# Mixer and gate weights split once beside the feed-forward quads and kept in DRAM; ten instead of twelve buffers for weight tiles; another order of stores and loads

## What is computed

```python
x = x + 0.5 * swiglu(rms_norm(x, ffn1_norm), ffn1_w_gu, ffn1_w_down)      # D_FF = 2816
h = rms_norm(x, mix_norm)
q, k, v, u = split(h @ w_in)                       # 8 query heads, 2 kv heads of 64, pool width 512
a = sliding_window_attention(norm(q), norm(k), v, rel_bias, sinks)        # window 128
m = multiscale_pool(u, pool_w, pool_scale)
x = x + concatenate([a, m]) @ w_out
x = x + 0.5 * swiglu(rms_norm(x, ffn2_norm), ffn2_w_gu, ffn2_w_down)
gate = sigmoid(rms_norm(x, ple_norm) @ ple_w_gate + ple_b_gate)
e = rms_norm(p @ ple_w_proj, ple_post_norm)
return x + gate * e
```

## Time and profile before

| | us |
|---|---|
| median of 3 runs | 1740.52 (1740.1 to 1742.68) |
| the profiled execution, its time | 1737.11 |
| the profiled execution, its span | 1735.3 |
| PE busy | 1684.5 (97% of the span) |
| DVE busy | 1255.8 (72%) |
| ACT busy | 698.6 (40%) |
| POOL busy | 233.7 (13%) |

### The profile page before, as it was taken

One profiled execution on the slowest core, in us unless ns is written; L12 is line 12 of the kernel. 1 busy time (PEld: TensorE's weight loads), 2 busy tenths in 40 slices (PEclk: granted clock), 3 DMA queues, 4 the chain that ended last, 5 costly groups with the idle time before them and its releaser, 6 DMA issues.

```text
span 1735.3 us, 20459 instructions
## 1 busy us (share of the span) xinstructions
PE 1684.5 (97%) x7348; PEld 1371.6 (79%) x7348; DVE 1255.8 (72%) x1794; ACT 698.6 (40%) x1121; POOL 233.7 (13%) x245
## 2 busy tenths in 40 slices
PE   6999999999899999999999999999999999999998
PEld 4878877888788888776677788888888888888877
DVE  6888686767756768687877788777667755676785
ACT  5533232322345444356655443232223234534442
POOL 0012222222100000044140001221212300000000
PEclk9999999999999999999999999999999999999999
DMA  8135554554579765121123213454445439876533
GB/s 292 55 140 188 176 194 174 214 176 176 176 239 317 218 193 161 61 63 58 42 66 121 87 64 128 176 189 169 169 159 188 164 128 302 273 243 190 167 105 121
DMA packets 127784, 282.95 MB, mean 163 GB/s; under 512 B 10523, under 2 KB 52164, under 8 KB 119364
## 3 DMA queue, kind: packets, MB, share of 16 engines
q1 hardware_dynamic: 124376, 275.57, 47.4%
q10 hardware_dynamic: 3308, 6.08, 0.9%
HBM read 204.52 MB, written 78.66 MB: 163 GB/s over the span
## 4 chain that ended last, share of the span: by engine, by line
PE 61%; DMA 15%; DVE 13%; POOL 5%; ACT 4%; issue 3%; SPq 0%; ACTq 0%; DVEq 0%; POOLq 0%
PE bank L861 20%; PE bank L862 19%; PE bank L863 19%; DMA wdr<-in_wd 9%; POOL wdr L843 5%; DMA wdc<-wdr 3%; DVE qb L1902 1%; DVE hn L1521 1%; PE bank L1107 1%; ACT probs L1445 1%; DVE w_lo L1736 1%; DVE probs L1914 1%; DVE dn_lo L1728 1%; DMA e_dram<-et 1%; DMA e_dram<-e_acc 1%
## 5 line engine op out<-in xcount | busy, mean ns | idle before, releaser
L861 PE MATMUL bank<-h_hi,t_hi 128*128 128x512 f32 x704 | 274.9, 390 | 0.5 <-ACT p L1239 0.5
L862 PE MATMUL bank<-h_lo,t_hi 128*128 128x512 f32 x704 | 273.9, 389 | 0.0
L863 PE MATMUL bank<-h_hi,t_lo 128*128 128x512 f32 x704 | 273.9, 389 | 0.0
L843 POOL TENSOR_TENSOR wdr<-wdr 128x256 f32<-128x256 f32 x176 | 168.7, 959 | 748.0 <-DMA wdr<-in_wd 737.6
L1728 DVE TENSOR_TENSOR dn_lo<-d_f,dn_hi 128x1024 fp32r<-128x1024 f32 x154 | 185.1, 1221 | 116.0 <-ACT dn_hi L1256 115.7
L861 PE MATMUL bank<-dn_hi 128*128 128x512 f32 x616 | 241.1, 391 | 0.6 <-DVE dn_lo L1728 0.6
L862 PE MATMUL bank<-dn_lo,dn_hi 128*128 128x512 f32 x616 | 239.7, 389 | 0.0
L863 PE MATMUL bank<-dn_hi,dn_lo 128*128 128x512 f32 x616 | 239.7, 389 | 0.0
L861 PE MATMUL bank<-c_hi,t_hi 128*128 128x512 f32 x544 | 213.0, 392 | 10.4 <-DVE c L1600 9.0
L1256 ACT ACTIVATE dn_hi<-d_f 128x1024 fp32r<-128x1024 f32 x154 | 159.9, 1056 | 151.7 <-DMA d_f<-in_wd 78.2
L862 PE MATMUL bank<-c_lo,t_hi 128*128 128x512 f32 x544 | 212.2, 390 | 0.0
(11 more groups left out here) (163 smaller groups left out, 2491.2 us busy)
## 6 DMA issues: line engine op xcount, KB each, us to landing
raw<-in_gu SPq DMA_DIRECT2D x44, 1024.0 KB, 6.0
d_f<-actc SPq DMA_DIRECT2D x154, 256.0 KB, 3.2
actc<-acts SPq DMA_DIRECT2D x20, 1792.0 KB, 7.8
raw_m<-in_units SPq DMA_DIRECT2D x52, 512.0 KB, 4.1
wdr<-in_wd SPq DMA_DIRECT2D x44, 512.0 KB, 5.4
wdc<-wdr SPq DMA_DIRECT2D x44, 512.0 KB, 3.4
d_f<-wdc SPq DMA_DIRECT2D x88, 256.0 KB, 3.2
d_f<-in_wd SPq DMA_DIRECT2D x66, 256.0 KB, 4.4
```

What stands on the lines that cost most here:

```text
L843: pool.tensor_tensor(blocks[to], blocks[one], blocks[two], ALU.add).then_inc(wd_made, 1)
L861: pe.matmul(ps, whi, vhi, start=first, stop=False, skip_group_check=onto)
L862: pe.matmul(ps, whi, vlo, start=False, stop=False, skip_group_check=onto)
L863: return pe.matmul(ps, wlo, vhi, start=False, stop=last, skip_group_check=onto)
```

## The change

Four things:

1. The 26 distinct `units` tiles of mixer and gate are split once. SP loads one per turn in turns 2 to 19 of feed-forward 1 and 2 to 9 of feed-forward 2 (`split_load`), ACT rounds it at the end of its quad and DVE subtracts it in the next quad, and SP stores both halves (2 x 512 KB) into a DRAM tensor `hl` in the next turn (`split_store`). Mixer and gate then load hi and lo ready made (2 x 512 KB for each of the 52 uses), straight into the four slots; ACT and DVE have no weight work there.
2. `TR` goes from 12 to 10; the freed 8 KB hold `unit_f`/`unit_low` (one place) and `unit_rounded`.
3. In a turn, `act_store` comes first, then `split_store`, then the piece of e; the turns with two chunks become 6, 8, 12, 14.
4. At the start, the small constants are loaded ahead of x, the second projection tile is split later, the projection's result has 8 instead of 4 buffers (`NET`), and the first norm sum comes after the fifth tile. In the quads, DVE adds the e tile later in its order.

```diff
-TR = 12
+TR = 10
-WD_TWO = (6, 10, 14, 17)
+WD_TWO = (6, 8, 12, 14)
+NET = 8
+N_SPLIT = N_IN + 2 * KT
+SPLITS = [list(range(N_IN + KT)), list(range(N_IN + KT, N_SPLIT))]
...
             def unit_load(n):
-                if n >= NRAW:
-                    sp.wait_ge(unit_split, n - NRAW + 1)
-                sp.dma_start(raw_m[n % NRAW][:, 0:size], src).then_inc(raw_in[n % NRAW], 16)
+                if slot_free(n):
+                    sp.wait_ge(main_made, slot_free(n))
+                else:
+                    sp.wait_ge(gu_made, NGU if n < U_GATE else 2 * NGU)
+                    sp.wait_ge(unit_out, 32 * (len(SPLITS[0]) if n < U_GATE else N_SPLIT))
+                s = (n - U_MIX) % SLOTS
+                sp.dma_start(plain(w_hi[s][:, :]), hl[mix_unit(n) - W_IN][:, 0:UNIT]).then_inc(w_in[s], 16)
+                sp.dma_start(plain(w_lo[s][:, :]), hl[mix_unit(n) - W_IN][:, UNIT:2 * UNIT]).then_inc(w_in[s], 16)
+
+            def split_load(u):
+                if u:
+                    sp.wait_ge(unit_out, 32 * u)
+                sp.dma_start(unit_f[:, :], units[W_IN + u]).then_inc(unit_in, 16)
+
+            def split_store(u):
+                sp.wait_ge(unit_lo, u + 1)
+                sp.dma_start(hl[u][:, 0:UNIT], plain(unit_rounded[:, :])).then_inc(unit_out, 16)
+                sp.dma_start(hl[u][:, UNIT:2 * UNIT], plain(unit_low[:, :])).then_inc(unit_out, 16)
...
+                    if q % 2 == 0:
+                        act_store(ph, q // 2 - 1)
+                    if 0 < q - U_QUAD <= len(SPLITS[ph]):
+                        split_store(SPLITS[ph][q - U_QUAD - 1])
                     if ph == 0 and 0 <= q - E_QUAD <= 2 * KT:
                         n = q - E_QUAD
...
-                    if q % 2 == 0:
-                        act_store(ph, q // 2 - 1)
...
-                    for c in WD_TURN.get(q, ()):
-                        wd_chunk(ph, c)
+                    for j, c in enumerate(WD_TURN.get(q, ())):
+                        wd_load(ph, c)
+                        if j == 0 and 0 <= q - U_QUAD < len(SPLITS[ph]):
+                            split_load(SPLITS[ph][q - U_QUAD])
+                        wd_store(ph, c)
...
+            def round_unit(u):
+                act.wait_ge(unit_in, 16 * (u + 1))
+                act.activation(unit_rounded[:, :], unit_f[:, :], ACT.Copy).then_inc(unit_hi, 1)
...
                     gate1(ph, q)
                     if ph == 0 and 0 <= q - E_QUAD < 2 * KT:
                         e_squares(q - E_QUAD)
+                    if 0 <= q - U_QUAD < len(SPLITS[ph]):
+                        round_unit(SPLITS[ph][q - U_QUAD])
...
+                if 0 <= q - U_QUAD - 1 < len(SPLITS[ph]):
+                    split_unit(SPLITS[ph][q - U_QUAD - 1])
...
-                if kind in ("win", "wout") and SLOTS <= MIXU_AT[step] + LATE:
-                    m = MIXU_AT[step] + LATE
-                    if m < N_MIXU:
-                        round_unit(U_MIX + m)
```

More of the change, by code:

```diff
@@ L58 @@
 W_GATE = W_OUT + KT
-NRAW = 2
 N_MIXU = 2 * N_IN + 2 * KT
@@ L65 @@
 LAG = 5
-LATE = SLOTS - 1
 P1, P2, Q6, Q7, Q5, Q4, Q3 = range(7)
@@ L259, with program @@
 H_AT = {2: 0, 3: 1, 6: 2, 7: 3}
-def program(nc, xT, pT, units, gu, wd, poolw, small, const, onehot, rel, band_row, band, e_dram, actc, wdc, x1, out):
+def program(nc, xT, pT, units, gu, wd, poolw, small, const, onehot, rel, band_row, band, hl, e_dram, actc, wdc, x1, out):
     with ExitStack() as ctx:
@@ L1198, in round_s @@
                     act.wait_ge(gu_made, ph * NGU + FIRST)
-                elif what == ("s", Q5, 0) and ph == 0:
-                    for i in range(4):
-                        act.wait_ge(e_out[i], 16 * (2 * KT // 4))
+                elif what == ("h", 1, 0) and ph == 0:
+                    for i in range(NET):
+                        act.wait_ge(e_out[i], 16 * (2 * KT // NET))
                 act.activation(operand("hi", what), source(what), ACT.Copy).then_inc(s_rounded, 1)
@@ L1366, in _ @@
             round_pj(0)
[L1367 removed]
             act.wait_ge(small_in, 16)
[L1369 to L1370 removed]
             for n in range(2 * KT):
                 e_tile(n)
[L1373 to L1383 removed]
+                if n == 0:
+                    x_square(0, 0)
+                    x_square(0, 1)
+                    round_pj(1)
+                elif n < 4:
+                    x_square(0, 2 * n)
+                    x_square(0, 2 * n + 1)
+                elif n == 4:
+                    std(0)
+                elif n in (5, 6):
+                    round_first(0, n - 5)
+                    if n == 6:
+                        round_first(0, 2)
+                elif n - 7 < KT:
+                    round_s(0, "h", 0, n - 7)
+                else:
+                    round_first(0, 3)
             act.wait_ge(band_made, 1)
@@ L1693, in quad @@
                 todo = [(q + 1, s) for s in LOS1] if more else []
-                if ph == 0 and 0 <= q - E_QUAD - 1 < 2 * KT:
-                    e_accumulate(q - E_QUAD - 1)
                 if q == 2:
                     split_t(ph, *todo[0])
-                if more:
+                elif more:
                     add_t(ph, q + 1, 0)
@@ L1708, in quad @@
                 make_w3(ph, q)
-                for x in todo[1:3]:
+                for x in todo[1 + (q == 2):3]:
                     split_t(ph, *x)
@@ L1991, in build @@
     x1 = nc.dram_tensor("x1", (D_MODEL, SEQ), F32, kind="Internal").ap()
-    program(nc, xT, pT, units, gu, wd, poolw, small, const, onehot, rel, band_row, band, e_dram, actc, wdc, x1, out)
+    program(nc, xT, pT, units, gu, wd, poolw, small, const, onehot, rel, band_row, band, hl, e_dram, actc, wdc, x1, out)
 def constants():
```

133 lines of the change are left out of this document (59 added, 74 removed).

## The result

The changed kernel takes 1767.43 us (median of 4 runs, 1766.68 to 1768.71), the kernel before in the same session 1740.31 us (4 runs, 1737.71 to 1742.68). The ratio is 1.0158, 95% interval 1.0138 to 1.0178. The profiled execution of after has a span of 1766.9 us and a mean granted clock of 0.983, against 1735.3 us and 0.992.

The account below looks back on a forecast made before the run. PE was busy 1684.5 of 1735.3 us; in feed-forward 1 SP's serial chain of load, POOL and store set SP's pace. -4 + 41 + 1 - 12 - 2 = +24 on 1740.5 gave about 1764 us, range 1731 to 1787.

Parts of the forecast that it names:

- The first quads, +41: Quads of feed-forward 1: unit stores ahead of `wdr` cost 2.9 us per turn, quads 41 us longer (+31 to +54).
- what would make me wrong: Sign against the forecast in SP's turns: they wait for `unit_lo` rather than for POOL; no size given.
- rival C: Unit landing, ACT's rounding, DVE's subtraction and store loop with SP; quads cost 54 to 70, total 1780 to 1800; chance 0.13.
- The forecast of PE's waits: First 530 us: PE waits on `c` and `p` by 40 us and more, in stalls after the double turns.
- Feed-forward 2, +1: Quads of feed-forward 2: SP waits for DVE each turn, so 2.9 us fit; +1 us (0 to +6).
- The mixer, -12: Mixer: weight work leaves ACT and DVE, half of PE's waits go; -12 us (0 to -25).
- The start, -4: Start: the 4.7 us on `et` and part of the clock should go; -4 us (0 to -7).
- gate, -2: Gate: PE's wait of 2.6 us on `sig` mostly goes; -2 us.
- down products, 0: Down products: PE did not wait there, so the five units that leave each change nothing.
- The upper bound's 3.4 us per turn: Quads of feed-forward 1: the highest cost per turn taken, 16 x 3.4, giving the bound of +54 us.
- A: Unit stores hide, quads cost nothing and recover up to 11 us; total 1712 to 1723, say 1720; chance 0.17.
- B: Costs and gains meet: 2.4 us per turn, mixer gains 20, sum +5; total 1733 to 1746, say 1742; chance 0.13.

Follow-up runs that it names:

- experiment 2: Changed kernel without the store of `unit_low`, 512 KB of the 1024 KB per unit; the high half is loaded in its place: 1732.25 us.
- experiment 3: Changed kernel with a third 512 KB store per unit, `unit_low` once more to a spare tensor: 1797.3 us.
- experiment 5: Changed kernel with ACT's rounding and DVE's subtraction on a filled scratch, not waiting for the unit's load; the plain unit is stored twice: 1777.47 us.
- experiment 10: Kernel before with only the new order: `actc` stored ahead of e, DVE's sum over e later, double turns 6, 8, 12, 14: 1740.67 us.
- experiment 12: Changed kernel with `wdr` loaded ahead of the unit's stores, double turns 8 and 14, and the band's broadcast moved to the down stage: 1713.71 us.
- experiment 1: Changed kernel with the load of `wdr` put ahead of the two unit stores in each turn of SP: 1739.15 us.
- experiment 7: Changed kernel with two turns of two chunks (8, 14) in place of four (6, 8, 12, 14): 1730.52 us.
- experiment 8: Changed kernel with `wdr` loaded ahead of the unit's stores and two double turns (8, 14) for four: 1714.98 us.
- Experiment 4: Changed kernel with ACT copies and DVE subtractions put back into the mixer as dummies on a scratch nobody reads: 1790.47 us.

## Why the prediction was right, and where only the sum was

**The first quads, +41: right, +44.7.** SP's turns grew by 2.73 us (2.9 forecast), the store of turn 18 came at 479.2 us (483), the stops of PE came on `p` after the double turns. Experiments 2 and 3 show the price of the bytes, 5 that ACT's wait for the unit is not the cause, 10 that the new order is not. To the first store of an even turn it took mostly 20.4 to 21.0 us (21 to 22 forecast), of an odd turn 15.8 to 17.4 (16 forecast). One stop more, in quad 5, came from the band (experiment 12). Two things in that step were incomplete. First, the 2.73 us are not all bytes ahead of `wdr`, and that they are so near 2.9 is in part luck. In turn 9 `wdr` was under way 9.2 us instead of 5.57, more than the price of the bytes. In turn 8 it was under way only 1.2 us longer than its like in the earlier trace rows, but was issued 5.2 us after the store ahead of it instead of 3.4, since SP waited for DVE's subtraction. And POOL's additions, which the sum left as they were, gave over a microsecond back in these turns. I had named SP waiting for `unit_low` as what would make me wrong; with 27.6 us against 139.7 for POOL it is the smaller part, but it is there, and it is the ring of rival C in a mild form. Second, the waits are 33 of the 45 us and the clock behind them 12. Since I had worked from SP's pace, not from PE's waits, the sum held the clock without naming it. The forecast of PE's waits, 40 us and more on `c` and `p`, was met by 42.7, nearly all of them on `p`.

**Feed-forward 2, +1: wrong, +17.9.** The step that failed is "Here SP does wait for DVE each turn, so 2.9 us fit". Of before it was true in the main: between 1063 and 1200 us SP waited 21.6 us for DVE, in five places. After, in turn 6 of feed-forward 2, the activations (1792 KB) and the two unit stores stand ahead of `wdr`, and it is 10.39 us under way, by the chain:

```profile
1153.16 10.39 DMA wdr<-in_wd
...
1167.28 3.05 DMA wdc<-wdr
1170.35 3.79 DMA wdr<-in_wd
...
1181.42 9.84 DMA hl<-unit_low
1191.28 3.51 DMA unit_f<-in_units
```

The double turns 6 and 8 then hit a loop with little left over, and PE stopped twice, 27.9 and 28.1 us for a quad of 19.0. I had SP "up to 15 us late" there and did not ask what that does to ACT, which by my own count for feed-forward 1 can be late by 7 us only. Experiments 1, 2, 7 and 8 each remove most of it (430.4, 428.7, 429.3, 425.4).

**The mixer, -12: mis-sized, -26.9.** The bound of -25 was the better value, and even it was passed. The term that was mis-sized is the half of PE's idle time that I let stand, on the ground that a unit's 1.2 us stands only now and then in the chains of attention. (The count was off too: 32 roundings and 32 subtractions lie in the mixer, 326 to 294 and 438 to 406 instructions in the rows above, not 36.) Measured, PE idle time fell from 17 to 1.3 us, and with the stops went the time at the lower clock, 11 us. Experiment 4 puts 21.9 of the 26.9 us on the work.

**The start, -4: -1.1; gate, -2: -3.3; down products, 0: +0.2 and 0.** At the start PE's waits on `et` fell only from 4.7 to 2.1 us, and 1.3 us came on at another wait (`acc`, 0.7 to 2.0). `TR` = 10 and ACT's and DVE's extra work in the quads were put at 0; no stop of PE names them, but neither was run by itself. The upper bound's 3.4 us per turn, in the forecast of the first quads, stands in no row.

**The rivals.** A, that the unit stores hide, is out by experiments 2 and 3. A total like B's came only in experiment 1. C, at 1780 to 1800, did not come, though its ring is in the chain; experiment 3 shows how near it is: 512 KB more per turn give 1797.

## What to carry to other kernels

- A serial chain (load, add, store) that shares one queue with something new pays for the new bytes most where they stand ahead of its load (28 us here). Put the link that everything waits for first, then look for the wait that takes its place: here it was the round trip through the one buffer of the newcomer.
- When a chain's turn and PE's come close, count the turns that carry double work and the one-off transfers. Spreading two chunks over turns that had none was worth more than the order here (36.9 us against 28.3), and 14.3 us in the kernel before too; measure the old kernel with the same cure before crediting the change.
- Price a short stop of PE at the wait plus the stretch at the lower clock behind it, and moved work at what its new place has to spare: the band gave 10 us in one stage and took 9 in the next.

## What I had not expected of the hardware

- The clock's share of a stop: in the first quads 12 us of busy time on 33 of idle, in the mixer 11 on 16. After a wait of 7.56 us the matmuls followed each other every 0.43 us for 4.8 us.
- POOL's additions of 128x256 took 0.74 us where DVE was idle and 1.07 us where it was at work, and so gave back part of what the late load of `wdr` cost.
- The near-linearity: 512 KB more or less of stores in SP's queue are 1.4 or 1.5 us per turn, wherever the wait behind it is put down.
